# A second ring of four raw units for the value product of a PEER layer on one NeuronCore

## What is computed

```
q = (h @ w_q).reshape(B, T, PEER_HEADS, 2, PEER_DHALF)
s = einsum('bshid,hikd->bshik', q, sub_keys)          # keys on both sides
... top 16 per side, top 16 of their 256 sums, softmax: idx, g
act = gelu(einsum('cd,ced->ce', hc, u[ic]))
wts = gc * act
out = einsum('ce,ced->cd', wts, v[ic])
...
return rms_norm(x + g2 * peer(h2), final_norm)
```

## Time and profile before

| what | value |
|---|---|
| median of three runs | 2227.6 us |
| the profiled execution | 2224.07 us |
| its span on the core | 2221.9 us |
| TensorE (PE) busy | 2108.7 us, 95% |
| VectorE (DVE) busy | 1672.5 us, 75% |
| ScalarE (ACT) busy | 1212.7 us, 55% |
| GpSimd (POOL) busy | 301.7 us, 14% |
| read from and written to DRAM | 515.52 MB, 8.39 MB |
| mean rate over the span | 236 GB/s |
| loads of units (raw<-stream) | 648 of 512 KB, 4.4 us in the middle from issue to landing |

### The profile page before, as it was taken

One profiled execution on the slowest core, in us unless ns is written; L12 is line 12 of the kernel. 1 busy time (PEld: TensorE's weight loads), 2 busy tenths in 40 slices (PEclk: granted clock), 3 DMA queues, 4 the chain that ended last, 5 costly groups with the idle time before them and its releaser, 6 DMA issues.

```text
span 2221.9 us, 42631 instructions
## 1 busy us (share of the span) xinstructions
PE 2108.7 (95%) x13442; PEld 1852.3 (83%) x13442; DVE 1672.5 (75%) x2954; ACT 1212.7 (55%) x2243; POOL 301.7 (14%) x264
## 2 busy tenths in 40 slices
PE   4899999898999999999999999999699999999996
PEld 0478888667989999999999999999487787777875
DVE  5477767787666588878786778877488888888886
ACT  2232235485445576776766565565365556565652
POOL 0000000000000000000001111111355452222220
PEclk7899999899999999999999999999899999999997
DMA  9878876400765455555697644444689999999992
GB/s 386 335 277 285 278 258 246 142 1 1 268 233 183 148 180 182 185 180 180 202 363 267 207 153 160 160 153 163 230 312 341 331 339 338 333 331 349 337 330 96
DMA packets 160890, 524.72 MB, mean 236 GB/s; under 512 B 34960, under 2 KB 35776, under 8 KB 160192
## 3 DMA queue, kind: packets, MB, share of 16 engines
q1 hardware_dynamic: 123840, 452.63, 57.3%
q0 software_dynamic: 20576, 67.20, 8.8%
q10 hardware_dynamic: 16416, 4.19, 0.9%
HBM read 515.52 MB, written 8.39 MB: 236 GB/s over the span
## 4 chain that ended last, share of the span: by engine, by line
PE 71%; DMA 16%; DVE 7%; issue 3%; ACT 2%; POOL 1%; SPq 0%; DVEq 0%; ACTq 0%
PE PS L720 60%; DMA raw<-stream 13%; PE PS L1033 3%; PE PS L977 2%; DVE w_lo L1070 2%; DMA ada_t<-w_ada 2%; DMA values_scratch<-A 1%; ACT w_hi L412 1%; PE PS L876 1%; DVE st L1271 1%; PE PS L850 1%; PE PS L763 1%; PE PS L727 1%; PE PS L703 1%; POOL picked L388 1%
## 5 line engine op out<-in xcount | busy, mean ns | idle before, releaser
L412 ACT ACTIVATE w_hi<-raw 128x512 fp32r<-128x512 f32 x1296 | 805.2, 630 | 822.3 <-PE PS L720 547.3
L1070 DVE TENSOR_TENSOR w_lo<-raw,w_hi 128x512 fp32r<-128x512 f32 x1296 | 865.8, 689 | 386.3 <-ACT w_hi L412 368.2
L720 PE MATMUL PS<-h_h,w_hi 128*128 128x256 f32 (+1 forms) x2304 | 657.6, 285 | 3.1 <-DVE h_l L1100 2.1
L720 PE MATMUL PS<-h_h,w_lo 128*128 128x256 f32 (+1 forms) x2304 | 652.9, 283 | 0.0
L720 PE MATMUL PS<-h_l,w_hi 128*128 128x256 f32 (+1 forms) x2304 | 652.8, 283 | 0.0
L720 PEld LDWEIGHTS PS<-h_h,w_hi 128*128 128x128 f32 x2304 | 442.8, 192 | 4.2 <-issue 2.6
L720 PEld LDWEIGHTS PS<-h_l,w_hi 128*128 128x128 f32 x2304 | 442.9, 192 | 0.0
L720 PEld LDWEIGHTS PS<-h_h,w_lo 128*128 128x128 f32 x2304 | 442.7, 192 | 0.0
L720 PE MATMUL PS<-w_hi,p_hl 128*128 128x512 f32 x1024 | 405.0, 396 | 31.1 <-DVE w_lo L1070 29.5
L720 PEld LDWEIGHTS PS<-w_hi,p_hl 128*128 128x128 f32 x1024 | 193.2, 189 | 88.9 <-issue 46.7
L720 PE MATMUL PS<-w_lo,p_hl 128*128 128x512 f32 x512 | 200.6, 392 | 0.0
(11 more groups left out here) (226 smaller groups left out, 2657.5 us busy)
## 6 DMA issues: line engine op xcount, KB each, us to landing
raw<-stream SPq DMA_DIRECT2D x648, 512.0 KB, 4.4
ada<-w_ada SPq DMA_DIRECT2D x96, 512.0 KB, 4.7
ada_t<-w_ada SPq DMA_DIRECT2D x64, 512.0 KB, 9.1
ada_u<-w_ada SPq DMA_DIRECT2D x32, 512.0 KB, 5.7
values_scratch<-A ACTq DMA_DIRECT2D x1, 2560.0 KB, 19.0
x_c<-x_ctx SPq DMA_DIRECT2D x1, 2048.0 KB, 7.8
x<-x_lat SPq DMA_DIRECT2D x1, 2048.0 KB, 15.1
x_scratch<-x SPq DMA_DIRECT2D x1, 2048.0 KB, 7.2
```

The lines of the kernel that those rows point to most:

```text
L412: nc.scalar.activation(w_hi[:, (2 * j + hf) % SPLIT, :], raw[:, j, hf * HALF:(hf + 1) * HALF], ACT.Copy).then_inc(S["w_high"], 1)
L720: ins = mm(out_, l_, r_, start=(start and q == 0), stop=(stop and q == 2), skip_group_check=check)
L1070: V_.tensor_tensor(w_lo[:, h % SPLIT, :], raw[:, h // 2 % RAW, at_:at_ + HALF], w_hi[:, h % SPLIT, :].bitcast(F32), ALU.subtract).then_inc ...
```

## The change

A second ring, `raw_far`, of four raw units (16 KB a partition) lies where tiles 8 to 23 of A were. From quadruple 111 on (`FAR_AT`, 12 turns of the value product later, `FAR_TURN`) quadruples go to the two rings in turn: 111 to the far one, 112 to the near one, and so on to 161, which is far. SyncE waits once for the tiles to be left (`values_kept`, `p_low` and `p_high_too` at 24), and each unit then waits for the unit eight places back. ScalarE's one loop of 63 turns is now one of 12, one of 25 passes of two turns, and a last turn. VectorE's loop over the first group of 16 turns is written out, because the ring changes within it. The reload of `x2` moves from before quadruple 148 to before 149. `raw_in[j]` and the new `far_in[j]` count the landings of their own ring.

```diff
+        far_in = [ctx.enter_context(nc.semaphore(f"far_in{i}")) for i in range(RAW)]
...
+        raw_far = at("raw_far", [P, RAW, UNIT], F32, R + 8 * KB)
...
-            with sp.Fori(42 + LATE_ADA_AT, X2_AT) as b:
+            with sp.Fori(42 + LATE_ADA_AT, FAR_AT) as b:
                 units(b)
+            sp.wait_ge(S["values_kept"], 32)
+            sp.wait_ge(S["p_low"], 24)
+            sp.wait_ge(S["p_high_too"], 24)
+            def unit_far(b, j):
+                sp.wait_ge(S["w_low"], 8 * b + 2 * (j - 7))
+                sp.dma_start(raw_far[:, j, :], stream[4 * b + j]).then_inc(far_in[j], 16)
+            def unit_near(b, j):
+                sp.wait_ge(S["w_low"], 8 * b + 2 * (j - 7))
+                sp.dma_start(raw[:, j, :], stream[4 * b + j]).then_inc(raw_in[j], 16)
+            def both_rings(b0, n):
+                with sp.Fori(0, n) as m:
+                    for j in range(RAW):
+                        unit_far(2 * m + b0, j)
+                    for j in range(RAW):
+                        unit_near(2 * m + (b0 + 1), j)
+            both_rings(FAR_AT, (X2_AT - FAR_AT) // 2)
             sp.wait_ge(S["p_low"], 80)
             sp.dma_start(x2[:], x2_dram).then_inc(S["x2_in"], 16)
-            with sp.Fori(X2_AT, U_END // 4) as b:
-                units(b)
+            both_rings(X2_AT, (U_END // 4 - 1 - X2_AT) // 2)
+            for j in range(RAW):
+                unit_far(U_END // 4 - 1, j)
...
+            def split_high_far(b, j, m):
+                act.wait_ge(far_in[j], 16 * m + 16)
+                half_high(b, j, 0, raw_far)
+                half_high(b, j, 1, raw_far)
+            def split_high_near(b, j, m):
+                act.wait_ge(raw_in[j], 16 * m + 16 * FAR_AT)
                 half_high(b, j, 0)
                 half_high(b, j, 1)
...
-            with act.Fori(0, N_V // 4 - 1) as b:
...
+            with act.Fori(0, FAR_TURN) as b:
+                value_turn(b, 0)
+            with act.Fori(0, (62 - FAR_TURN) // 2) as m:
+                value_turn_into_far(m)
+                value_turn_into_near(m)
+            value_turn_into_far((62 - FAR_TURN) // 2)
+            split_high_far(161, 2, (62 - FAR_TURN) // 2)
+            split_high_far(161, 3, (62 - FAR_TURN) // 2)
...
+            def ring_of(b):
+                return raw_far if b >= FAR_AT and (b - FAR_AT) % 2 == 0 else raw
...
+                if g == 0:
+                    for r in range(bodies):
+                        for s in range(4):
+                            value_turn(0, 3 + 4 * r + s, r, s)
+                    continue
...
-X2_AT = 148
+FAR_TURN = 12
+FAR_AT = 99 + FAR_TURN
+X2_AT = 149
```

More of the change, by code:

```diff
@@ L409, in _, with half_high @@
         def _(act):
-            def half_high(b, j, hf):
+            def half_high(b, j, hf, ring=raw):
                 act.wait_ge(S["w_free"], 8 * b + (2 * j + hf + 1))
-                nc.scalar.activation(w_hi[:, (2 * j + hf) % SPLIT, :], raw[:, j, hf * HALF:(hf + 1) * HALF],
+                nc.scalar.activation(w_hi[:, (2 * j + hf) % SPLIT, :], ring[:, j, hf * HALF:(hf + 1) * HALF],
                                      ACT.Copy).then_inc(S["w_high"], 1)
@@ L417, in split_high @@
                 act.wait_ge(raw_in[j], 16 * b + 16)
+                half_high(b, j, 0)
+                half_high(b, j, 1)
+            def split_high_far(b, j, m):
[4 more added lines that the diff above has]
+                act.wait_ge(raw_in[j], 16 * m + 16 * FAR_AT)
                 half_high(b, j, 0)
@@ L672, in _, with value_turn, value_turn_into_far, value_turn_into_near @@
             p_high(1, 1)
-            with act.Fori(0, N_V // 4 - 1) as b:
[L674 to L681, removed]
+            def value_turn(b, b0):
+                split_high(b + (98 + b0), 2)
+                split_high(b + (98 + b0), 3)
+                p_high(2 * b + (2 * b0 + 2), 0)
+                split_high(b + (99 + b0), 0)
+                split_high(b + (99 + b0), 1)
+                p_high(2 * b + (2 * b0 + 3), 1)
+            def value_turn_into_far(m):
+                split_high_near(2 * m + (FAR_AT - 1), 2, m)
+                split_high_near(2 * m + (FAR_AT - 1), 3, m)
+                p_high(4 * m + (2 * FAR_TURN + 2), 0)
+                split_high_far(2 * m + FAR_AT, 0, m)
+                split_high_far(2 * m + FAR_AT, 1, m)
+                p_high(4 * m + (2 * FAR_TURN + 3), 1)
+            def value_turn_into_near(m):
+                split_high_far(2 * m + FAR_AT, 2, m)
+                split_high_far(2 * m + FAR_AT, 3, m)
+                p_high(4 * m + (2 * FAR_TURN + 4), 0)
+                split_high_near(2 * m + (FAR_AT + 1), 0, m + 1)
+                split_high_near(2 * m + (FAR_AT + 1), 1, m + 1)
+                p_high(4 * m + (2 * FAR_TURN + 5), 1)
+            with act.Fori(0, FAR_TURN) as b:
[6 more added lines that the diff above has]
+            split_high_far(161, 3, (62 - FAR_TURN) // 2)
             act.wait_ge(S["v_done"], 1)
@@ L1064, in link, with half_low, split_low @@
                 dve.wait_ge(S["dve"], chain["n"])
-            def half_low(b, h):
+            def half_low(b, h, ring=raw):
                 dve.wait_ge(S["w_high"], 8 * b + (h + 1))
                 at_ = (h % 2) * HALF
-                V_.tensor_tensor(w_lo[:, h % SPLIT, :], raw[:, h // 2 % RAW, at_:at_ + HALF],
+                V_.tensor_tensor(w_lo[:, h % SPLIT, :], ring[:, h // 2 % RAW, at_:at_ + HALF],
                                  w_hi[:, h % SPLIT, :].bitcast(F32), ALU.subtract).then_inc(S["w_low"], 1)
-            def split_low(b, j):
-                half_low(b, 2 * j)
-                half_low(b, 2 * j + 1)
+            def split_low(b, j, ring=raw):
+                half_low(b, 2 * j, ring)
+                half_low(b, 2 * j + 1, ring)
             def ada_add(c, kt, last):
@@ L1593, in mix @@
                                         mixed[:, cols], ALU.mult, ALU.add).then_inc(S["mixed"], 1)
+            def ring_of(b):
+                return raw_far if b >= FAR_AT and (b - FAR_AT) % 2 == 0 else raw
             def value_turn(b, b0, r=None, s=0):
-                split_low(b + (98 + b0), 2)
-                split_low(b + (98 + b0), 3)
+                split_low(b + (98 + b0), 2, ring_of(98 + b0))
+                split_low(b + (98 + b0), 3, ring_of(98 + b0))
                 if r is not None:
@@ L1601, in value_turn @@
                 p_low(2 * b + (2 * b0 + 2), 0)
-                split_low(b + (99 + b0), 0)
-                split_low(b + (99 + b0), 1)
+                split_low(b + (99 + b0), 0, ring_of(99 + b0))
+                split_low(b + (99 + b0), 1, ring_of(99 + b0))
                 if r is not None:
@@ L1629, in _ @@
                         value_turn(4 * r, 3 + g * PICK_GROUP + s, r + g * (PICK_GROUP // 4), s)
-            split_low(161, 2)
-            split_low(161, 3)
+            split_low(161, 2, ring_of(161))
+            split_low(161, 3, ring_of(161))
             for s in range(4):
```

## The result

The changed kernel takes 2205.9 us (median of four, 2202.8 to 2209.1) against 2228.3 (four runs): ratio 0.9898, 95% interval 0.9881 to 0.9915, 22.4 us less. Its profiled execution took 2209.09 us, 15.0 less than the profiled one before. In the comparison of the first four experiments one of 17 executions of the kernel before took 4166.6 us, which nothing here explains; it is left out of every median and ratio.

A forecast was written before the change was run, and what follows sets the result against it. The ring of four's landing loop was taken to delay TensorE in the value product: 20.5 us lost, less 1.2 to build the lead, is 19.3; nine tenths, 17.4, off 2227.6 gives 2210.2 us, range 2206 to 2221.

The forecast's parts named there:

- What bounds it: value product: a ring of four cannot turn faster than its 9.40 us loop, against TensorE's 9.07 us per turn.
- The ring of eight, and whether the engines can carry it: from quadruple 111: 15.9 us left for a landing; traffic 347 GB/s against 410 moved at the stage's head, 63 to spare.
- 20.5 us of the 485 are lost: value product, 1690 to 2175 us: 2049 matmuls need 464.5 us; 20.5 us is the most to regain.
- It now costs 4.6 us: reload of x2, window 2020 to 2050 us: 25.4 us of work in 30 us; 4.6 us counted as regained.
- The lead must be built: start of the far ring: four more units take 33 us, 3.7 turns, to get ahead, so 1.2 us are not recovered.
- Nine tenths: of the 19.3 us sum only 17.4 taken, the tenth an allowance for bursts that a mean rate does not show.
- Reload regained whole: unit behind the x2 reload has 15.9 us and needed 9.61, so all 4.6 us come back.
- waits on SyncE: before SyncE's new loop: waits for weighted tiles and stored values are already past on arrival, cost 0.
- VectorE, ScalarE, picked rows at 0: value stage: VectorE at 8.45 us per turn, ScalarE's two-turn loop and later-landing picked rows each cost 0.
- little to spare: rival, chance 0.15: engines' limit 365 GB/s, lead takes 117 us to build, half of 20.5 returns, 2217 us.
- no gain: rival, chance 0.08: rows and units together bear at most 336 GB/s, landings grow, time 2227 us.
- Code that is not there: rival, chance 0.05: instruction fetches for ScalarE's longer loop or VectorE's written-out turns wait behind a full queue; 2235 us.

The follow-up runs named there:

- the first four experiments: the changed kernel again, 2206.1 us, then with each unit waiting for the one four, five or six places back: 2228.4, 2210.8, 2204.7 us.
- leads of 3, 4, 5 and 6: changed kernel, but a unit waits for the unit that many places back, not eight: 2322.7, 2228.4, 2210.8 and 2204.7 us.
- the runs with more traffic: changed kernel with one or two more 512 KB loads per turn from quadruple 117, into memory nobody reads: 2206.2 and 2263.2 us.
- the kernel before with the reload in pieces: kernel before, ring of four, x2 reloaded in eight 256 KB pieces ahead of every second unit of quadruples 148 to 151: 2222.3 us, ratio 0.9975.
- the kernel with the mixes later: changed kernel with the first mix of a picked row two turns later, in the sixth turn: 2195.5 us, ratio to the kernel before 0.9848.
- four and few rows: kernel before, ring of four, picked rows from row 16 on fetched as two 128 x 128 pieces instead of 128 x 1024: 2209.6 us.

## Why the prediction was as it was, point by point

- *What bounds it*: right. A loop of landing, w_hi, w_lo and issue longer than TensorE's turn; leads of 3, 4, 5 and 6 follow it.
- *The ring of eight, and whether the engines can carry it*: right. Every turn is 9.07; the forecast was some 345 GB/s and the window shows 353; the limit is 410.
- *"20.5 us of the 485 are lost. That is the most that this change can give back"*: **this step failed**, by its size, and with it the low end of the range (2206.0), which was the whole 20.5 and 1 us of spread. It was the loss of one trace, and of three traces of that kernel the smallest: the same stage lost 1.0 and 3.8 us more in two other executions. From the first split of quadruple 111 the three give 19.9, 20.9 and 23.7 us, 21.5 in the mean.
- *"It now costs 4.6 us"* (the reload): the term of that sum that was too low. Over turns 146 to 149 that trace loses 5.2 us, the other two 8.6 and 7.3, as the late unit needed 13.0 and 11.5 us in place of 9.61; the mean is 7.0. The other turns, 14.8 us in that trace, are 14.5 in the mean of three.
- *The lead must be built, 1.2 us*: wrong. ScalarE waited once more, for 1.8 us, and turns 110 and 111 took 9.11. SyncE issued the four far units in a burst of 2.39 us, and they lay ready by the time they were needed:

```profile
1691.45 2.39 SPq L342 DMA_DIRECT2D raw_far<-stream  x4
```

- *Nine tenths*: wrong, 1.9 us. No tenth was lost: TensorE never stands in the 465 us, and every turn takes its 9.07. Of the 5.0 us between the forecast gain and the measured one these two deductions are 3.1, the one trace is 1.0 (20.5 to 21.5), and the 0.9 us between 21.5 and 22.4 are within the interval (18.9 to 26.5).
- *The range*: that the median lies 0.1 us below it and not above is chance; when the changed kernel was run again its median was 2206.1. What is not chance is that the gain is 5 us above the forecast one.
- *Reload regained whole, waits on SyncE, VectorE, ScalarE, picked rows at 0*: right; ScalarE waits for TensorE, and VectorE for ScalarE but for 0.9 us.
- *The other ways*: little to spare and no gain are out by the runs with more traffic. Code that is not there: the lead of four, with all the new code, is 1.0002 of before; no wait for code beyond measuring. Of idle time put to issue ScalarE has 21 times 0.5 us in the stage. It is not the new loop's: the kernel before with the reload in pieces, whose ScalarE code is the old one, has 15 such, and TensorE is busy throughout the 465 us beside the 21.

## What to carry to other kernels

In this kernel a ring was long enough if its slots, at the pace of the engine that should set the time, covered a landing and the steps around it. Work that sum out with the slowest landing, and first of all with the one behind a large load in the same queue. A large load can be cut in pieces before memory is spent on slots; here that alone gave 5 to 6 us. And a bound read from one trace is a draw: where a rare event carries a quarter of it, as the reload does here, take its spread from further traces, or widen the range by it.

## What the runs showed that I had not expected

- **The low clock behind a stand is not of one length.** Between 1200 and 1240 us both kernels run the same instructions (the product with U, ahead of the change), with one stand of TensorE, of 1.6 us in both. Before and changed:

```profile
1200.00:1240.00 40.00, 38.36 (x311) 38.18 (x310) 20.30 (x40) 22.75 (x36) 12.89 (x8) 0.96 0.60 178
```
```profile
1200.00:1240.00 40.00, 38.36 (x298) 38.19 (x297) 19.34 (x36) 21.89 (x35) 11.56 (x7) 0.91 0.51 165
```

  Granted clock 0.96 and 0.91, 13 matmuls apart. VectorE's splits are 1.6 us later behind it, and with two such places further ahead (2.2 and 1.5 us) this makes the 5.3 us by which this trace of the changed kernel is late at the value product. It is chance: another kernel of the same code (lead of six) came there 3.5 us earlier. The traces of this study, whose kernels run the same instructions up to there, reach the value product up to 9.1 us apart, which is about the spread between executions of one kernel (8.5 us for the changed one).
- **Landings did not get shorter with fewer units in flight while the rows were there**: in the middle 6.3 us with a lead of three, 6.1 to 6.3 with four (kernel before), 6.7 to 6.8 with eight (the kernel with the mixes later), 8.5 with eight at 407 GB/s, and 4.3 with four and few rows.
